# Modulation columns by transposes, and up products over high and low activations side by side

## The chip, the cores and the metric

One NeuronCore of one Trainium2 chip runs the whole program. The metric is the device time of one execution in microseconds (us), the median of several runs.

## What is computed

Two transformer blocks of two layers each, on 256 tokens of 1024 features, all in float32. The part that the change touches is the MLP, which stands in each of the four layers (and once more for the context stream of the second block, five in all), and the modulation of the second block:

```python
def hybrid_layer(...):                       # first block, two layers
    ...
    u = rms_norm(x, ln2) @ w_up              # 1024 -> 4096
    return x + jnp.square(jax.nn.relu(u)) @ w_down

def second_block(x, c, ctx, c_ctx, ...):     # two layers
    ctx_s = ctx
    for l in range(DEPTH):
        mod = (jax.nn.silu(c) @ w_mod[l] + b_mod[l])[:, None, :]
        mod_c = (jax.nn.silu(c_ctx)[None] @ w_mod[l] + b_mod[l])[:, None, :]
        sh1, sc1, gt1, sh2, sc2, gt2 = jnp.split(mod, N_MOD, axis=-1)
        ...
        x = x + gt1 * merge_branches(...)
        x = x + gt2 * sq_relu_mlp(modulate(x, g_norm2[l], sh2, sc2), w_ff1[l], w_ff2[l])
```

## The kernel before

**Precision.** Every large product is made of three in a fast float32 format (`F32R`): a value is split into a high part, rounded to the format, and a low part, the rest. A weight chunk is one load of 1 MB (128 partitions x 2048 values) into one of six `RAW` buffers. ScalarE casts it to the high part in one of four `HI` buffers (line 619), VectorE subtracts to get the low part `LO` (line 1114), which overwrites `RAW`. Activations are kept as `AH` and `AL`, each 8 blocks of 128 features by 256 tokens. TensorE then adds high x high, high x low and low x high in PSUM.

**The MLP** (`mlp` on TensorE, ScalarE and VectorE) has four rounds i of eight chunks j. The chunks j = 0 to 3 hold up weights, 256 hidden features each. `features_out` makes them: two halves q of 128 features, and for each the 8 blocks of input features, three products of 256 columns (lines 1805 to 1807), into half a PSUM bank, 4 or 5 in turn. ScalarE takes the relu (line 751) and its square, rounded, as `HIDH`; VectorE takes relu times value as `U2` and the rest as `HIDL` (lines 1231, 1235). The chunks j = 4 to 7 hold down weights, each 24 products of 512 columns (`tokens_out`, lines 1763 to 1765). `PS` is the whole of PSUM, eight banks of 512 values a partition. For early input of the next stage banks 6 and 7 take transposes in round 3.

**Order.** Each engine's program is written out by hand. At each chunk c ScalarE and VectorE first run `ahead(c)`, the split of chunk c + 3, and then the work on what TensorE made of chunk c. `s_used` counts chunks that TensorE has ended, `s_lo` splits that are done, `s_ufree` banks that are free, `s_hl` low parts of hidden features. SyncE issues the load of chunk c + 6 when chunk c is used.

**Modulation.** 24 groups of 512 columns of `w_mod`. `mod_chunk` (line 1838, or `modulation`, line 1972) makes two rows (the two streams) in one bank with four column tiles: the 1024 input features are spread over them, so that rows 0 and 1 of each of four blocks of 32 partitions hold partial sums. ScalarE copies the bank to `ROWS` or `ROWS4`. Then `mod_column` (line 1846) makes columns of them: four products of `ROWS` with the constant selector `SEL` (128 x 2), which adds the four blocks and leaves 2 columns for each 128 features, 8 in one bank. VectorE adds the bias into `MOD` (line 1187). Two groups come before a stage, two or three in the second block's gate chunks, one in some MLPs; at the end of each layer of the first block four come together, all in bank 3, behind the first half group of the output projection `c_o` (lines 2077 to 2082 on TensorE, 1467 to 1473 on VectorE), with TensorE waiting for `s_modc` before the third.

The selector is the last of twelve constants that ScalarE loads before its first work.

Of the kernel before, what the change touches and what calls it, by code (L numbers as in the profile page):

```python
# [15 lines left out]
P = 128  # L16
D = 1024
KT = D // P
# [117 lines left out]
MT_BANK = (1, 0, 1)  # L136

# [72 lines left out]
def build(nc, a, out):  # L210

    with ExitStack() as ctx:
# [20 lines left out]
        AH = sb("AH", [P, KT, S], F32R)  # L233
        AL = sb("AL", [P, KT, S], F32R)
# [20 lines left out]
        SEL = sb("SEL", [P, 2])  # L255
# [141 lines left out]
        s_so = sem("output_gate")  # L397
        s_rl = sem("hidden_relu")
# [114 lines left out]
        NCH = LP.end  # L513

# [102 lines left out]
        def _(act):  # L617
# [29 lines left out]
            const(SEL[:, :], a["selector"])  # L647
# [40 lines left out]
            def high(n, scale=None, shift=None, steps=range(4)):  # L688

                for s in steps:  # L690
                    act.wait_ge(s_tp, n + s - steps[0] + 1)
                    dst = AH[:, 2 * s:2 * s + 2, :].rearrange("p a n -> p (a n)")
                    if scale is None:
                        cast(dst, PS[:, 6 + s % 2, :]).then_inc(s_thi, 1)
                        continue

                    whole = vector_scales(s, shift)
                    out = dst if whole else TMP[:, s % 2, :]
                    for j in range(2):
                        last = nc.scalar.activation(out[:, 256 * j:256 * j + 256],  # L700
# [3 lines left out]
                    if whole:  # L704
                        last.then_inc(s_thi, 1)
                    else:
                        link(last)
                        cast(dst, TMP[:, s % 2, :]).then_inc(s_thi, 1)
# [22 lines left out]
            def mlp(q, c, u, late=NO_SLOT):  # L731

                e = EARLY.get(q)
                for i in range(4):
                    for j in range(8):
                        ahead(c + 8 * i + j + late.n)
# [11 lines left out]
                        if j < 4:  # L748

                            act.wait_ge(s_used, c + 8 * i + j + late.n + 1 + HL_N)  # L750
                            nc.scalar.activation(RL[:, j % 2, :], PS[:, 4 + (u + j) % 2, :], ACT.Relu).then_inc(s_rl, 1)  # L751
# [343 lines left out]
        def _(dve):  # L1095
# [34 lines left out]
            def low(n, scale=None, shift=None, steps=range(4)):  # L1130

                for s in steps:
                    d = 2 * s
                    hi = AH[:, d:d + 2, :].rearrange("p a n -> p (a n)").bitcast(F32)
                    lo = AL[:, d:d + 2, :].rearrange("p a n -> p (a n)")

                    dve.wait_ge(s_thi, n + s - steps[0] + 1)
                    full = PS[:, 6 + s % 2, :] if scale is None else TMP[:, s % 2, :]
                    if scale is not None and shift is not None and vector_scales(s, shift):
# [4 lines left out]
                    if scale is not None and shift is None:  # L1144
                        for j in range(2):
                            last = stt(lo[:, 256 * j:256 * j + 256], PS[:, 6 + s % 2, 256 * j:256 * j + 256],
                                       scale(d + j), hi[:, 256 * j:256 * j + 256], ALU.mult, ALU.subtract)
# [36 lines left out]
            def mod_column(g, bank):  # L1184

                l, k = g // 12, 4 * (g % 12)
                tt(MOD[:, l, k:k + 4, :], PS[:, bank, 0:8].rearrange("p (c s) -> p c s", s=2),
                   PAR[:, 128 + 48 * l + k:132 + 48 * l + k].unsqueeze(2).to_broadcast((P, 4, 2)),
# [20 lines left out]
            def mlp(q, c, u, m, later=None):  # L1209

                e = EARLY.get(q)
                for i in range(4):
                    for j in range(8):
                        ahead(c + 8 * i + j + m.n)
# [11 lines left out]
                        if j < 4:  # L1226
# [25 lines left out]
            for l in range(DEPTH):  # L1252
# [443 lines left out]
        def _(pe):  # L1696
# [112 lines left out]

            def group(g, c, n=512):  # L1810
# [31 lines left out]

# [511 lines left out]
```

## Time and profile before

| | |
|---|---|
| median of 3 runs | 1882.28 us (1881.24 to 1882.91) |
| the profiled execution | 1882.55 us |
| its span, first to last instruction | 1880.7 us |
| TensorE busy | 1816.5 us, 97% |
| VectorE, ScalarE busy | 1104.7 us, 59%; 916.1 us, 49% |
| granted clock of TensorE, mean | 0.987 of full |
| moved by DMA | 342.49 MB, mean 182 GB/s |

Busy time of TensorE overlaps from one matmul to the next: the time between two starts is shorter than the duration that is printed. In names of the trace the two activation buffers are AH and AL. A matmul in plain float32, such as one with `SEL`, stands as two records. A window's clock is a share of full speed, 2.4 GHz; 0.50 is the lower level, 1.2 GHz.

### The profile page before, as it was taken

What the parts mean: (1) busy time and instruction counts of PE and PEld (TensorE: products, weight loads), DVE (VectorE), ACT (ScalarE), POOL (GpSimd) and SP (SyncE); (2) the same over time, 40 slices, a digit from 0 to 9 for tenths busy, and PEclk for the clock granted to TensorE, in tenths of its full rate; (3) what the DMA queues carried; (4) which work ended last, traced back from release to release, by engine and by line L of the source; (5) the groups of instructions that cost most, each with busy time, mean ns of one, the idle gap of its engine ahead of it and who ended that gap; (6) DMA issues with size and microseconds to landing.
All of it is one profiled execution on the core that took longest, in us unless ns stands there. A gap on an engine that the chain in (4) does not pass through costs nothing.

```text
span 1880.7 us, 26344 instructions
## 1 busy us (share of the span) xinstructions
PE 1816.5 (97%) x11210; PEld 1562.8 (83%) x11210; DVE 1104.7 (59%) x1247; ACT 916.1 (49%) x1211; POOL 38.4 (2%) x32
## 2 busy tenths in 40 slices
PE   7899999998899999999999999999999999999998
PEld 6768999796689998778899997778999787779997
DVE  3866555466655545357655564686555655676554
ACT  5454444453454445465544544555444545654442
POOL 0000000000000000000000000000000000000000
PEclk9999999999999999999999999999999999999999
DMA  7464565653656657564656555636565656355562
GB/s 245 135 207 152 186 195 180 219 161 125 215 178 187 194 179 247 201 207 142 212 185 195 180 180 196 206 113 202 183 195 183 224 165 216 113 179 157 180 195 73
DMA packets 228236, 342.49 MB, mean 182 GB/s; under 512 B 9908, under 2 KB 118808, under 8 KB 227992
## 3 DMA queue, kind: packets, MB, share of 16 engines
q1 hardware_dynamic: 226928, 339.45, 55.5%
q8 instruction: 89, 1.46, 0.3%
q10 hardware_dynamic: 1192, 1.36, 0.2%
q14 instruction: 27, 0.22, 0.0%
HBM read 339.74 MB, written 1.05 MB: 181 GB/s over the span
## 4 chain that ended last, share of the span: by engine, by line
PE 91%; DVE 5%; ACT 2%; issue 1%; POOL 1%; ACTq 0%; DVEq 0%; POOLq 0%
PE PS L1763 15%; PE PS L1765 14%; PE PS L1764 14%; PE PS L1805 9%; PE PS L1806 9%; PE PS L1807 9%; PE PS L2131 1%; PE PS L2179 1%; PE PS L2133 1%; PE PS L2132 1%; PE PS L2202 1%; PE PS L2190 1%; PE PS L1838 1%; PE PS L2151 1%; PE PS L2149 1%
## 5 line engine op out<-in xcount | busy, mean ns | idle before, releaser
L1114 DVE TENSOR_TENSOR LO<-RAW,HI 128x2048 fp32r<-128x2048 f32 (+1 forms) x274 | 621.4, 2276 | 413.6 <-ACT HI L619 412.8
L619 ACT CAST HI<-RAW 128x2048 fp32r<-128x2048 f32 (+1 forms) x274 | 516.5, 1891 | 266.4 <-PE PS L1765 225.6
L1805 PE MATMUL PS<-AH,HI 128*128 128x256 f32 x1424 | 409.3, 287 | 9.0 <-DVE AL L1561 7.9
L1806 PE MATMUL PS<-AL,HI 128*128 128x256 f32 x1424 | 407.9, 286 | 0.0
L1807 PE MATMUL PS<-AH,LO 128*128 128x256 f32 x1424 | 407.6, 286 | 0.0
L1805 PEld LDWEIGHTS PS<-AH,HI 128*128 128x128 f32 x1424 | 278.7, 196 | 11.3 <-issue 9.8
L1806 PEld LDWEIGHTS PS<-AL,HI 128*128 128x128 f32 x1424 | 278.6, 196 | 0.6
L1807 PEld LDWEIGHTS PS<-AH,LO 128*128 128x128 f32 x1424 | 278.4, 196 | 0.0
L1763 PE MATMUL PS<-HI,AH 128*128 128x512 f32 (+2 forms) x704 | 257.7, 366 | 0.0
L1765 PE MATMUL PS<-HI,AL 128*128 128x512 f32 (+2 forms) x704 | 252.0, 358 | 0.0
L1764 PE MATMUL PS<-LO,AH 128*128 128x512 f32 (+2 forms) x704 | 251.6, 357 | 0.0
L1763 PE MATMUL PS<-HI,HIDH 128*128 128x512 f32 x640 | 250.1, 391 | 0.0
L1764 PE MATMUL PS<-LO,HIDH 128*128 128x512 f32 x640 | 249.3, 389 | 0.0
L1765 PE MATMUL PS<-HI,HIDL 128*128 128x512 f32 x640 | 249.1, 389 | 0.0
L1763 PEld LDWEIGHTS PS<-HI,AH 128*128 128x128 f32 x704 | 137.6, 195 | 32.4 <-issue 14.3
L751 ACT ACTIVATE RL<-PS 128x512 f32<-128x512 f32 x80 | 47.8, 597 | 221.6 <-PE PS L1807 217.7
L1765 PEld LDWEIGHTS PS<-HI,AL 128*128 128x128 f32 x704 | 137.3, 195 | 19.1
L1764 PEld LDWEIGHTS PS<-LO,AH 128*128 128x128 f32 x704 | 137.8, 196 | 17.9 <-issue 0.5
L1765 PEld LDWEIGHTS PS<-HI,HIDL 128*128 128x128 f32 x640 | 120.2, 188 | 25.0
L1763 PEld LDWEIGHTS PS<-HI,HIDH 128*128 128x128 f32 x640 | 120.2, 188 | 24.2
L1764 PEld LDWEIGHTS PS<-LO,HIDH 128*128 128x128 f32 x640 | 120.3, 188 | 24.1
L1231 DVE SCALAR_TENSOR_TENSOR U<-PS,RL 128x512 f32<-128x512 f32 x80 | 55.3, 691 | 89.0 <-ACT RL L751 88.8
(269 smaller groups left out, 1862.4 us busy)
## 6 DMA issues: line engine op xcount, KB each, us to landing
RAW<-in_w_ff SPq DMA_DIRECT2D x96, 1024.0 KB, 5.4
RAW<-in_w_in SPq DMA_DIRECT2D x80, 1024.0 KB, 5.2
RAW<-in_w_mod SPq DMA_DIRECT2D x48, 1024.0 KB, 5.1
RAW<-in_w_up SPq DMA_DIRECT2D x32, 1024.0 KB, 5.5
RAW<-in_w_down SPq DMA_DIRECT2D x32, 1024.0 KB, 5.0
RAW<-in_w_o SPq DMA_DIRECT2D x12, 1024.0 KB, 5.0
RAW<-in_w_out SPq DMA_DIRECT2D x8, 1024.0 KB, 5.6
RAW<-in_w_attn_out SPq DMA_DIRECT2D x6, 1024.0 KB, 5.3
```

The costliest lines, as they stand in the source:

```text
L619: return nc.scalar.copy(dst, src)
L751: nc.scalar.activation(RL[:, j % 2, :], PS[:, 4 + (u + j) % 2, :], ACT.Relu).then_inc(s_rl, 1)
L1114: tt(LO[:, c % RAW_N, 0:n], RAW[:, c % RAW_N, 0:n], HI[:, NTH[c] % HL_N, 0:n].bitcast(F32), ALU.subtract).then_inc(s_lo, 1)
L1231: stt(U2[:, j % 2, :], PS[:, 4 + (u + j) % 2, :], 0.0, RL[:, j % 2, :], ALU.max, ALU.mult).then_inc(s_ufree, 1)
L1763: mm(o, th, hi[:, j, :], start=first and j == 0, stop=False)
L1764: mm(o, th, lo[:, j, :], start=False, stop=False)
L1765: ins = mm(o, tl, hi[:, j, :], start=False, stop=last and j == kt - 1)
L1805: mm(o, wh, ah[:, j, :], start=j == 0, stop=False)
L1806: mm(o, wh, al[:, j, :], start=False, stop=False)
L1807: ins = mm(o, wl, ah[:, j, :], start=False, stop=j == KT - 1)
L1838: last = mm(PS[32 * k:32 * k + 32, banks[j // 2], :], C32[:, 4 * (j % 2) + k, :], RAW[:, c % RAW_N, 512 * k:512 * k + 512], start=j % 2 == ...
L2131: mm(o, th, hi[:, j, cols], start=j == 0, stop=False)
```

## The change

1. `AH` and `AL` become two views of one tensor `AHL`, in which each block of features has its 256 high values and then its 256 low ones.
2. In each MLP all up chunks but the first two of round 0 use `features_wide`: per block of features one product of the high weights with the 512 columns of `AHL`, and one of the low weights with the 256 high columns, added to the first half of the bank. Each half q of the chunk has a bank of its own: 6 and 7 for even j, 4 and 5 for odd.
3. ScalarE copies the first halves of both banks to `U2` before it runs `ahead`, VectorE adds the second halves and frees the banks; relu and square then read `U2`.
4. `mod_column` transposes the four pieces of a row group with the identity into the whole bank, and VectorE sums the four blocks in a reduction and adds the bias. At the layers' ends the four groups go to banks 4, 5, 3 and 2. The selector and its load are gone.

```diff
+TAIL_BANKS = (4, 5, 3, 2)
...
-        AH = sb("AH", [P, KT, S], F32R)
-        AL = sb("AL", [P, KT, S], F32R)
+        AHL = sb("AHL", [P, KT, 2, S], F32R)
+        AH, AL = AHL[:, :, 0, :], AHL[:, :, 1, :]
...
+        def wide(i, j):
+
+            return i > 0 or j > 1
+
+        def copies(q, i, j):
+
+            return 14 * q + 4 * i + j - 1
+
+        def wide_banks(j):
+
+            return 4 if j % 2 else 6
...
-            const(SEL[:, :], a["selector"])
...
+                        if j < 4 and wide(i, j):
+
+                            b = wide_banks(j)
+                            act.wait_ge(s_used, c + 8 * i + j + late.n + 1 + HL_N)
+                            act.wait_ge(s_hl, 16 * q + 4 * i + j - 1)
+                            cast(U2[:, j % 2, :].rearrange("p (a n) -> p a n", a=2),
+                                 PS[:, b:b + 2, 0:256]).then_inc(s_up, 1)
                         ahead(c + 8 * i + j + late.n)
...
 
-                            act.wait_ge(s_used, c + 8 * i + j + late.n + 1 + HL_N)
-                            nc.scalar.activation(RL[:, j % 2, :], PS[:, 4 + (u + j) % 2, :], ACT.Relu).then_inc(s_rl, 1)
+                            if wide(i, j):
+                                act.wait_ge(s_ufree, u + 4 * i + j + 1 + 2)
+                                up = U2[:, j % 2, :]
+                            else:
+                                act.wait_ge(s_used, c + 8 * i + j + late.n + 1 + HL_N)
+                                up = PS[:, 4 + (u + j) % 2, :]
+                            nc.scalar.activation(RL[:, j % 2, :], up, ACT.Relu).then_inc(s_rl, 1)
                             act.wait_ge(s_rl, 16 * q + 4 * i + j + 1)
                             nc.scalar.activation(HIDH[:, j // 2, 2 * (j % 2):2 * (j % 2) + 2, :].rearrange("p a n -> p (a n)"),
                                                  RL[:, j % 2, :], ACT.Square).then_inc(s_hh, 1)
...
                 l, k = g // 12, 4 * (g % 12)
-                tt(MOD[:, l, k:k + 4, :], PS[:, bank, 0:8].rearrange("p (c s) -> p c s", s=2),
-                   PAR[:, 128 + 48 * l + k:132 + 48 * l + k].unsqueeze(2).to_broadcast((P, 4, 2)),
+                mod = MOD[:, l, k:k + 4, :]
+                parts = PS[:, bank, :].rearrange("p (c b r) -> p c r b", c=4, b=4)[:, :, 0:2, :]
+                link(nc.vector.tensor_reduce(mod, parts, AX_X, ALU.add))
+                tt(mod, mod, PAR[:, 128 + 48 * l + k:132 + 48 * l + k].unsqueeze(2).to_broadcast((P, 4, 2)),
                    ALU.add).then_inc(s_modc, 1)
 
...
                     for j in range(8):
+                        if j < 4 and wide(i, j):
+
+                            b = wide_banks(j)
+                            dve.wait_ge(s_up, copies(q, i, j))
+                            up = U2[:, j % 2, :].rearrange("p (a n) -> p a n", a=2)
+                            tt(up, up, PS[:, b:b + 2, 256:512], ALU.add).then_inc(s_ufree, 1)
                         ahead(c + 8 * i + j + m.n)
...
                             dve.wait_ge(s_rl, 16 * q + 4 * i + j + 1)
-                            stt(U2[:, j % 2, :], PS[:, 4 + (u + j) % 2, :], 0.0, RL[:, j % 2, :], ALU.max,
-                                ALU.mult).then_inc(s_ufree, 1)
-                            dve.wait_ge(s_ufree, u + 4 * i + j + 1 + 2)
+                            if wide(i, j):
+                                link(stt(U2[:, j % 2, :], U2[:, j % 2, :], 0.0, RL[:, j % 2, :], ALU.max, ALU.mult))
+                            else:
+                                stt(U2[:, j % 2, :], PS[:, 4 + (u + j) % 2, :], 0.0, RL[:, j % 2, :], ALU.max,
+                                    ALU.mult).then_inc(s_ufree, 1)
+                                dve.wait_ge(s_ufree, u + 4 * i + j + 1 + 2)
                             dve.wait_ge(s_hh, 16 * q + 4 * i + j + 1)
                             tt(HIDL[:, j // 2, cols:cols + 2, :].rearrange("p a n -> p (a n)"),
...
-                dve.wait_ge(s_mcol, L.m_o.g + 4)
                 for j in range(4):
-                    g = L.m_o.g + j
-                    tt(MOD[:, g // 12, 4 * (g % 12):4 * (g % 12) + 4, :],
-                       PS[:, 3, 8 * j:8 * j + 8].rearrange("p (c s) -> p c s", s=2),
-                       PAR[:, 128 + 48 * (g // 12) + 4 * (g % 12):132 + 48 * (g // 12) + 4 * (g % 12)].unsqueeze(2)
-                       .to_broadcast((P, 4, 2)), ALU.add).then_inc(s_modc, 1)
+                    dve.wait_ge(s_mcol, L.m_o.g + j + 1)
+                    mod_column(L.m_o.g + j, TAIL_BANKS[j])
                 gain = lambda k: PAR[:, 16 + 8 * l + k:17 + 8 * l + k]
...
+            def features_wide(c, b):
+
+                arrived(c)
+                hi, lo = slot(c, KT, 256)
+                for q in range(2):
+                    for j in range(KT):
+                        wh, wl = hi[:, j, 128 * q:128 * q + 128], lo[:, j, 128 * q:128 * q + 128]
+                        mm(PS[:, b + q, :], wh, AHL[:, j, :, :].rearrange("p a n -> p (a n)"), start=j == 0, stop=False)
+                        ins = mm(PS[:, b + q, 0:256], wl, AH[:, j, :], start=False, stop=j == KT - 1)
+                ins.then_inc(s_used, 1)
+
             def group(g, c, n=512):
...
+            def turn_rows(rows, bank):
+
+                for k in range(4):
+                    last = nc.tensor.transpose(PS[:, bank, 128 * k:128 * k + 128], rows[:, 128 * k:128 * k + 128], IDM)
+                last.then_inc(s_mcol, 1)
+
             def mod_column(j, bank):
 
-                for k in range(4):
-                    last = mm(PS[:, bank, 2 * k:2 * k + 2], ROWS[:, j, 128 * k:128 * k + 128], SEL[:, :],
-                              start=True, stop=True)
-                last.then_inc(s_mcol, 1)
+                turn_rows(ROWS[:, j, :], bank)
 
             def mod_columns(m, banks):
...
-                        features_out(c + 8 * i + j + (0 if first else m.n), 4 + (u + j) % 2, AH, AL,
-                                     ts if first else None, tiles if first else None, 1 + m.n if first else 1)
+                        if wide(i, j):
+                            features_wide(c + 8 * i + j + m.n, wide_banks(j))
+                        else:
+                            features_out(c + 8 * i + j + (0 if first else m.n), 4 + (u + j) % 2, AH, AL,
+                                         ts if first else None, tiles if first else None, 1 + m.n if first else 1)
                         if i == 0 and j == 1:
...
+                        if e and i == 3 and j == 0:
+                            pe.wait_ge(s_ufree, u + 4 * i + 2 + 1 + 2)
...
                     pe.wait_ge(s_mrow, L.m_o.g + j + 1)
-                    for k in range(4):
-                        last = mm(PS[:, 3, 8 * j + 2 * k:8 * j + 2 * k + 2], ROWS4[:, j, 128 * k:128 * k + 128],
-                                  SEL[:, :], start=True, stop=True)
-                    last.then_inc(s_mcol, 1)
+                    turn_rows(ROWS4[:, j, :], TAIL_BANKS[j])
                 half_group(L.c_o + 1, 0, 1, ts=ts)
```

How it stands in the order of the instructions, in three places.

TensorE at the start of an up chunk in layer 0's MLP (j = 2 of round 0), before; `AH` and `AL` are the activations:

```order
L1805 MATMUL PS<-AH,HI 128x256 [waits chunk_split_done,ubank_evacuated]
L1806 MATMUL PS<-AL,HI 128x256
L1807 MATMUL PS<-AH,LO 128x256
L1805 MATMUL PS<-AH,HI 128x256
L1806 MATMUL PS<-AL,HI 128x256
```

and in the changed program, the end of that chunk and the start of the next (j = 3):

```order
L1849 MATMUL PS<-AHL,HI 128x512
L1850 MATMUL PS<-AHL,LO 128x256
L1849 MATMUL PS<-AHL,HI 128x512 [waits chunk_split_done,ubank_evacuated]
L1850 MATMUL PS<-AHL,LO 128x256
L1849 MATMUL PS<-AHL,HI 128x512
L1850 MATMUL PS<-AHL,LO 128x256
```

The triple of 256 columns has become a pair of 512 and 256, and what a chunk waits for is the same.

ScalarE in the same round, before (j = 2 and 3):

```order
L619 CAST HI<-RAW 128x2048 [waits chunk_used,raw_loaded_4]
L751 ACTIVATE RL<-PS 128x512 [waits chunk_used]
L753 ACTIVATE HIDH<-RL 128x512 [waits hidden_relu]
L619 CAST HI<-RAW 128x2048 [waits chunk_used,raw_loaded_5]
L751 ACTIVATE RL<-PS 128x512 [waits chunk_used]
L753 ACTIVATE HIDH<-RL 128x512 [waits hidden_relu]
```

and now; `U_104` is `U2`:

```order
L632 COPY U_104<-PS 128x512 [waits hidden_low,chunk_used]
L632 CAST HI<-RAW 128x2048 [waits chunk_used,raw_loaded_5]
L775 ACTIVATE RL<-U_104 128x512 [waits ubank_evacuated]
L777 ACTIVATE HIDH<-RL 128x512 [waits hidden_relu]
L632 COPY U_104<-PS 128x512 [waits hidden_low,chunk_used]
L632 CAST HI<-RAW 128x2048 [waits chunk_used,raw_loaded_0]
L775 ACTIVATE RL<-U_104 128x512 [waits ubank_evacuated]
L777 ACTIVATE HIDH<-RL 128x512 [waits hidden_relu]
```

The copy out of the banks stands ahead of the split of a later chunk, which used to come before anything that waits for this chunk; the relu waits for VectorE.

TensorE at the end of layer 0, before: the last of the four groups of modulation columns (three like it stand above) and the start of the next half group of `c_o`; `ROWS_104` is `ROWS4`:

```order
L2080 MATMUL PS<-SEL,ROWS_104 128x2 [waits mod_rows_copied]
L2080 MATMUL PS<-SEL,ROWS_104 128x2 x3
L1763 MATMUL PS<-HI,AH 128x512 [waits activation_low,chunk_split_done]
L1764 MATMUL PS<-LO,AH 128x512
L1765 MATMUL PS<-HI,AL 128x512
```

and now, `CT` being the identity and `ROWS_102` the same `ROWS4`:

```order
L1889 MATMUL PS<-CT,ROWS_102 128x128 [waits mod_rows_copied]
L1889 MATMUL PS<-CT,ROWS_102 128x128 x3
L1795 MATMUL PS<-HI,AHL 128x512 [waits activation_low,chunk_split_done]
L1796 MATMUL PS<-LO,AHL 128x512
L1797 MATMUL PS<-HI,AHL 128x512
```

Sixteen transposes stand where the sixteen selector products stood.

## Rows read from the trace of the kernel before

**Rows 1.** The page before: parts 1 (busy us, share, instructions), 2 and 4.

```profile
PE 1816.5 (97%) x11210; PEld 1562.8 (83%) x11210; DVE 1104.7 (59%) x1247; ACT 916.1 (49%) x1211; POOL 38.4 (2%) x32
...
PEclk9999999999999999999999999999999999999999
...
PE 91%; DVE 5%; ACT 2%; issue 1%; POOL 1%; ACTq 0%; DVEq 0%; POOLq 0%
```

**Rows 2.** Timeline of ScalarE in an MLP: start us, us, engine line op out<-in.

```profile
1001.53 0.60 ACT L751 ACTIVATE RL<-PS 128x512 f32<-128x512 f32 x1 [3.79 <-PE PS L1807]
1002.16 0.63 ACT L753 ACTIVATE HIDH<-RL 128x512 fp32r<-128x512 f32 x1
1002.70 1.89 ACT L619 CAST HI<-RAW 128x2048 fp32r<-128x2048 f32 x1
1007.29 0.60 ACT L751 ACTIVATE RL<-PS 128x512 f32<-128x512 f32 x1 [2.70 <-PE PS L1807]
...
1029.77 1.91 ACT L619 CAST HI<-RAW 128x2048 fp32r<-128x2048 f32 x1 [3.53 <-PE PS L1765]
1035.21 1.91 ACT L619 CAST HI<-RAW 128x2048 fp32r<-128x2048 f32 x1 [3.53 <-PE PS L1765]
```

**Rows 3.** The same of VectorE.

```profile
1004.62 2.29 DVE L1114 TENSOR_TENSOR LO<-RAW,HI 128x2048 fp32r<-128x2048 f32 x1 [1.04 <-ACT HI L619]
1007.92 0.69 DVE L1231 SCALAR_TENSOR_TENSOR U<-PS,RL 128x512 f32<-128x512 f32 x1 [1.00 <-ACT RL L751]
1008.65 0.69 DVE L1235 TENSOR_TENSOR HIDL<-U,HIDH 128x512 fp32r<-128x512 f32 x1
```

**Rows 4.** Timeline of TensorE and VectorE around the modulation columns, x records.

```profile
150.93 3.63 PE L2080 MATMUL PS<-SEL,ROWS 128*128 128x2 f32 x32
154.42 0.48 PE L1763 MATMUL PS<-HI,AH 128*128 128x512 f32 x1
...
380.42 1.84 PE L1846 MATMUL PS<-SEL,ROWS 128*128 128x2 f32 x16
...
497.58 4.26 PE L2080 MATMUL PS<-SEL,ROWS 128*128 128x2 f32 x32
501.70 0.77 PE L1763 MATMUL PS<-HI,AH 128*128 128x512 f32 x1
...
501.87 0.38 DVE L1470 TENSOR_TENSOR MOD<-PS,PAR 128x8 f32<-128x8 f32 x4 [3.81 <-PE PS L2080]
...
515.27 1.03 PE L1735 MATMUL PS<-CT,X 128*128 128x128 f32 x8
...
800.02 0.95 PE L1846 MATMUL PS<-SEL,ROWS 128*128 128x2 f32 x8
```

**Rows 5.** Busy time by windows: us, PE, PEld, DVE, ACT, POOL, PEclk, DMA share, GB/s.

```profile
155.60:159.00 3.40, 3.40 (x9) 2.66 (x9) 1.58 (x1) 0.00 (x0) 0.00 (x0) 0.50 0.10 31
...
500.30:507.10 6.80, 6.80 (x22) 5.64 (x22) 2.58 (x5) 0.00 (x0) 0.00 (x0) 0.51 0.57 191
380.40:384.00 3.60, 3.60 (x33) 3.60 (x32) 0.33 (x2) 3.35 (x5) 0.00 (x0) 1.00 0.62 185
515.00:516.10 1.10, 1.10 (x11) 0.97 (x10) 0.71 (x1) 0.14 (x1) 0.00 (x0) 1.00 0.55 193
1289.00:1296.00 7.00, 6.20 (x30) 6.23 (x31) 7.00 (x5) 5.02 (x5) 0.00 (x0) 0.52 0.00 0
```

**Rows 6.** Timeline of SyncE's queue and of ScalarE at the end of layer 1.

```profile
501.94 0.37 SPq L581 DMA_DIRECT2D CTX<-in_ctx  x1
502.35 8.04 SPq L550 DMA_DIRECT2D RAW<-in_w_up  x3
...
510.56 1.91 ACT L619 CAST HI<-RAW 128x2048 fp32r<-128x2048 f32 x1 [10.83 <-DMA RAW<-in_w_up]
```

**Rows 7.** Timeline of the opening.

```profile
5.88 0.37 ACTq L633 DMA_DIRECT2D SEL<-selector  x1
6.29 1.28 ACT L684 ACT_TABLE_LOAD   x1 [6.29 <-issue]
```

More of the change, by code:

```diff
@@ L254, in build @@
         C32 = sb("C32", [P, KT, 32])
-        SEL = sb("SEL", [P, 2])
         SGC = sb("SGC", [P, 16])
@@ L397, in build @@
         s_so = sem("output_gate")
+        s_up = sem("hidden_part_copied")
         s_rl = sem("hidden_relu")
@@ L691, in high @@
                     act.wait_ge(s_tp, n + s - steps[0] + 1)
-                    dst = AH[:, 2 * s:2 * s + 2, :].rearrange("p a n -> p (a n)")
+                    dst = AH[:, 2 * s:2 * s + 2, :]
                     if scale is None:
-                        cast(dst, PS[:, 6 + s % 2, :]).then_inc(s_thi, 1)
+                        cast(dst, PS[:, 6 + s % 2, :].rearrange("p (a n) -> p a n", a=2)).then_inc(s_thi, 1)
                         continue
                     whole = vector_scales(s, shift)
-                    out = dst if whole else TMP[:, s % 2, :]
+                    out = dst if whole else TMP[:, s % 2, :].rearrange("p (a n) -> p a n", a=2)
                     for j in range(2):
-                        last = nc.scalar.activation(out[:, 256 * j:256 * j + 256],
+                        last = nc.scalar.activation(out[:, j, :],
                                                     PS[:, 6 + s % 2, 256 * j:256 * j + 256], ACT.Identity,
@@ L707, in high @@
                         link(last)
-                        cast(dst, TMP[:, s % 2, :]).then_inc(s_thi, 1)
+                        cast(dst, out).then_inc(s_thi, 1)
             def copy_group(pair, c, dst, n):
@@ L1133, in low @@
                     d = 2 * s
-                    hi = AH[:, d:d + 2, :].rearrange("p a n -> p (a n)").bitcast(F32)
-                    lo = AL[:, d:d + 2, :].rearrange("p a n -> p (a n)")
+                    hi = AH[:, d:d + 2, :].bitcast(F32)
+                    lo = AL[:, d:d + 2, :]
                     dve.wait_ge(s_thi, n + s - steps[0] + 1)
                     full = PS[:, 6 + s % 2, :] if scale is None else TMP[:, s % 2, :]
+                    full = full.rearrange("p (a n) -> p a n", a=2)
                     if scale is not None and shift is not None and vector_scales(s, shift):
@@ L1145, in low @@
                         for j in range(2):
-                            last = stt(lo[:, 256 * j:256 * j + 256], PS[:, 6 + s % 2, 256 * j:256 * j + 256],
-                                       scale(d + j), hi[:, 256 * j:256 * j + 256], ALU.mult, ALU.subtract)
+                            last = stt(lo[:, j, :], PS[:, 6 + s % 2, 256 * j:256 * j + 256], scale(d + j), hi[:, j, :],
+                                       ALU.mult, ALU.subtract)
                         last.then_inc(s_tlo, 1)
@@ L2325, in _ @@
                 mlp(q.mlp, q.c_mlp, q.u + 3, q.m_mlp, None, tiles=q.tile(1, 1, 0))
-N_CONST, N_ROWS = 12, 11
+N_CONST, N_ROWS = 11, 11
 INPUTS = ["x", "ln1", "w_in", "conv_w", "conv_b", "igate_b", "fgate_b", "mlstm_norm", "moba_q_norm", "moba_k_norm",
@@ L2347 @@
     args["constants"] = nc.dram_tensor("constants", table.shape, F32, kind="ExternalInput").ap()
-    pairs = np.tile(np.eye(32, 2, dtype=np.float32), (4, 1))
-    arrays["selector"] = pairs
-    args["selector"] = nc.dram_tensor("selector", pairs.shape, F32, kind="ExternalInput").ap()
     out = nc.dram_tensor("out", (1, S, D), F32, kind="ExternalOutput").ap()
```

## The prediction, made before the changed kernel ran

> **What bounds the kernel now.** I read the page first: TensorE is busy 97% of the span, VectorE 59%, ScalarE 49%, and the chain that ended last is 91% TensorE; the granted clock is near full in all slices [rows 1]. So a TensorE instruction that disappears is worth its own start-to-start time wherever TensorE isn't waiting, and work added to VectorE and ScalarE is free until it makes TensorE wait.
>
> Second, the timeline of ScalarE in one MLP, since its waits on TensorE mark where each weight chunk ends. Two relus stand 5.76 us apart, two casts of the down half 5.44 us apart [rows 2]. An up chunk is 48 matmuls of 256 columns, so 5.76/48 = 0.120 us each; a down chunk is 24 of 512 columns, so 5.44/24 = 0.2267 us each. Doubling the columns costs 0.1067 us (256 columns at the full level, 2.4 GHz), so both sizes carry the same 0.0133 us that doesn't depend on columns. The durations printed (0.28, 0.39 us) overlap and are not the cost; the spacing is.
>
> Third, the timeline of VectorE in the same place: per up chunk one LO subtraction of 2.29 us, the squared relu 0.69, the low part 0.69, with waits between [rows 3]. That is 3.7 of 5.76 us; ScalarE has 0.60 + 0.63 + 1.89 = 3.1.
>
> Fourth, TensorE around the modulation columns, and the granted clock there by windows [rows 4, 5].
>
> **The change, part by part.**
>
> *Wide up products.* In each MLP 14 of 16 up chunks become wide (all but i = 0, j = 0 and 1), 5 MLPs, 70 chunks. Before: 16 triples of 256 columns, 48 x 0.120 = 5.76. Now: 16 products of 512 columns and 16 of 256, in alternation, as the order shows. The columns streamed are the same 12,288; what goes is 16 fixed parts. Chunk: 16 x (0.2267 + 0.120) = 5.55 us, 0.213 less; 70 x 0.213 = **14.9 us**. The trace of before has no alternation of the two sizes. Bounds: a pair costs at most what the triple does, 0.360 (no gain), or at least its columns without a fixed part, 0.320 (0.64 us a chunk, 45 us in all). I take 0.3467, since both neighbours show the same fixed part [rows 2].
>
> *What the wide products add.* ScalarE copies one half out of two banks (nearest: relu of the same size, 0.60 us), VectorE adds the other (nearest: 0.69 us) [rows 2, 3]: 42 us and 48 us in all, at zero, because TensorE covers them. The check: TensorE may overwrite a bank pair only after the addition, two chunks later. Behind the end of a chunk come the copy 0.60 and the addition 0.69, some 1.4 us, plus at worst one LO subtraction that VectorE has in hand, 2.29: 3.7 us against 5.55 us of cover. The weights: ScalarE now waits for chunk c before it casts c+3, where before it had cast c+3 while c ran. Queued behind that wait are the HI cast (1.89) and then LO (2.29), so c+3 is ready about 0.6 + 1.9 + 2.3 = 4.8 us after c ends; TensorE wants it 11.1 us after. VectorE per wide chunk: 0.69 + 2.29 + 0.69 + 0.69 = 4.4 of 5.55. ScalarE: 3.7. If this cover went, TensorE would stop at the bank pair of the next wide chunk.
>
> *Modulation columns.* 24 groups. Each was four products with the selector, which the trace counts as 8 records (192 records for 96); now four transposes, which elsewhere are one record each. Eight transposes print 1.03 us where eight selector records print 0.95, sixteen 1.84 and 32 print 3.63 [rows 4]; 32 end 3.49 us on by the next start, so 0.14 of each print is overlap. One record or one transpose costs about 0.11 either way, and half the records is half the time. Ten single groups: 0.81 less half of 0.89, 0.365 each, 3.7 us. Three pairs: 1.70 - 0.89 = 0.81 each, 2.4 us. Two sets of four at the layers' ends: 3.49 - 1.78 = 1.71 each, 3.4 us. Sum **9.5 us**. Bounds: nothing gained, if a transpose of these rows costs two records, to 10.5 us, at 0.10 a transpose. On VectorE each group gains a reduction of 32 elements a partition and a link; four additions took 0.38 us together [rows 4], so I put a group at 0.3 us, anywhere from 0.1 to the 0.69 of a 512-column operation. Hidden: TensorE asks for the columns only after a half group of 5.44 us.
>
> *The clock at the layers' ends.* Right behind the 32 selector records the granted clock falls to its lower level, 1.2 GHz: from 155.6 to 159.0 us in layer 0, and from 500.3 to 507.1 us in layer 1, with TensorE busy all along [rows 5]. Half the stretch is lost: 1.7 and 3.4 us (in layer 1 that includes the 0.63 us by which its 32 records took longer, 4.12 against 3.49). What TensorE did before the fall was 3.5 us of two-column products. In the place where it did only 1.7 us of them, the clock stayed full [rows 4, 5]. The change leaves 1.78 us of 128-column transposes, so I take both falls as gone: **5.1 us**. Bounds: 0, and -5.1 if they get twice as long.
>
> *DMA queues.* SyncE holds the context's load and three w_up loads behind the last column of layer 1 [rows 6]; this comes 4.12 - 1.78 = 2.3 us earlier, and so do they. The cast of the second up chunk waited for that load until 510.56. TensorE ends the half group before it at 497.58 + 1.78 + 5.44 = 504.8, so the wait survives and lasts to about 508.3. It costs nothing: the cast and LO are done at 508.3 + 1.9 + 2.3 = 512.5, and TensorE gets to this chunk after two more half groups, eight transposes and a quarter of a chunk, at 504.8 + 10.9 + 0.9 + 1.4 = 518. The selector's load was the last of ScalarE's twelve, 0.41 us before its first activation [rows 7]; without it the opening is at most **0.4 us** earlier, at least 0 if x lands no sooner. I take 0.4.
>
> **Sum.** 14.9 + 9.5 + 5.1 + 0.4 = 29.9 us off the profiled execution's own 1882.55 us (span 1880.7 and 1.85 around it): **1852.6**. The median of the three runs, 1882.28, is 0.3 us lower, far inside the error. Stretches at the lower clock also stand behind waits at the passes' ends (1289 to 1296: mean clock 0.52 [rows 5]); they may shift with all that moves, each worth about 1.7 us, and I allow 3.5 us both ways.
>
> **Rivals.**
>
> *A, the clock still falls at the layers' ends.* No row shows sixteen transposes in one run between half groups. The sum loses 5.1: 1857.7. For it: the run of narrow work is halved, not gone. Against: eight selector pairs' worth, 1.7 us, and eight transposes leave the clock at full [rows 5].
>
> *B, wide products save nothing.* A pair costs 0.360, because a short product can't cover the fixed part of a long one. 1852.6 + 14.9 = 1867.5. Against: the equal fixed part at both sizes.
>
> *C, slower: transposes throw the clock down.* Columns are turned in 15 places, and each would then be followed by a stretch like layer 0's, 3.4 us long, 1.7 lost: 25.5 us. The transposes themselves would stream at half pace and gain nothing. 1882.55 - 14.9 - 0.4 + 25.5 = 1892.8. It decides from 9 of 15 places (9 x 1.7 = 15.3, what else is gained). Against it: at 515.27 eight transposes stand between half groups, and the clock of their window is 1.00 [rows 4, 5].
>
> The Trainium skill (TensorE: Matmul & The Clock Gate, Part 4: PE-mode transpose) states that full clock does not engage for transposes, which it says are not counted as busy in the same way. By that rule this change would trade one poor filler for another, and rival A or even C would hold. The trace does not bear out its strong form. No row says whether it holds weakly.
>
> *D, slower: the bank pairs.* If copy and addition ended later than the next chunk, TensorE would wait at each of 70 wide chunks. From 5.55 us on it costs; it eats all other gains from 6.0 us on (29.9/70 = 0.43). At 7 us it costs 1.45 x 70 = 101 us: 1852.6 + 101 = 1954. Worked out above at 3.7 at most, so it needs a stall that no row shows.
>
> That the change doesn't do what it says is excluded by the order: 70 chunks are in alternation and the selector has gone.
>
> **How the numbers follow.** The forecast 0.67; A 0.17; B 0.06; C 0.03; D 0.02; a small new wait somewhere of 3 to 8 us, 0.05. A measurement of this kernel tells about 0.2%, 3.8 us, from no change. All but C and D are faster by more; for the same I leave 0.01, for slower 0.05, faster 0.94. The range: from 1847 (the forecast with the clock kinder by 3.5 and a fixed part that shrinks a little) to 1862 (A with a small wait); B, C and D lie outside, some 0.12 to 0.15 with the tails. The one result above 1862 that I count likeliest is B.
>
> **What would show it.** Relus in the i = 1 rounds 5.55 us apart; 1120 products of 512 columns and 1120 of 256 in the new line, no wait of TensorE on the addition; 96 records of ROWS transposes, four in some 0.44 us; granted clock 1.00 in the windows behind them; an addition of about 0.69 us on VectorE and a copy of 0.60 on ScalarE, 70 of each. Wrong would be: a spacing of 5.7 or more (B), clock 0.5 behind the turned rows (A or C), TensorE idle before a wide chunk (D).

## The result, and the profile after

The changed kernel takes **1861.51 us** (median of 4 runs, 1859.63 to 1862.39), the kernel before 1882.57 us beside it (4 runs, 1881.24 to 1882.91): a ratio of 0.9888, interval 0.9871 to 0.9905. That is faster, by 21 us where 29.9 were forecast; the predicted time was 1852.6, the range 1847 to 1862. The profiled execution took 1862.11 us, its span 1860.3; against the 1882.55 from which the sum was made that is 20.4 us less.

The page of the changed kernel, the lines that answer to [rows 1], and from its part 5 the costliest groups of the new code (busy us, mean ns of one | idle before, releaser):

```profile
PE 1796.1 (97%) x9994; PEld 1488.6 (80%) x9994; DVE 1148.0 (62%) x1341; ACT 950.2 (51%) x1281; POOL 38.4 (2%) x32
...
PEclk9999999899999999999999999999999999999999
...
PE 89%; DVE 6%; ACT 2%; issue 1%; POOL 1%; DMA 1%; ACTq 0%; DVEq 0%; POOLq 0%
...
L1849 PE MATMUL PS<-AHL,HI 128*128 128x512 f32 x1120 | 396.2, 398 | 0.0
L1850 PE MATMUL PS<-AHL,LO 128*128 128x256 f32 x1120 | 314.3, 281 | 0.0
...
L632 ACT COPY U<-PS 128x512 f32<-128x512 f32 x70 | 41.1, 587 | 260.4 <-PE PS L1850 260.4
...
L1246 DVE TENSOR_TENSOR U<-U,PS 128x512 f32<-128x512 f32 x70 | 48.2, 688 | 136.8 <-ACT U L632 136.6
```

The change does what it says: 1120 wide and 1120 narrow products, 70 copies of 587 ns, 70 additions of 688 ns. TensorE has no idle time ahead of either product (0.0), so the 89 us of new work on ScalarE and VectorE cost nothing in the MLPs. Two things already differ from the plan: VectorE has 6% of the chain of waits where it had 5, and one slice of the granted clock shows an 8 where before none did.

The timeline of ScalarE in the same MLP as [rows 2] (start us, us, engine line op):

```profile
987.73 0.59 ACT L632 COPY U<-PS 128x512 f32<-128x512 f32 x1 [9.12 <-PE PS L1850]
988.21 1.91 ACT L632 CAST HI<-RAW 128x2048 fp32r<-128x2048 f32 x1
990.02 0.63 ACT L775 ACTIVATE RL<-U 128x512 f32<-128x512 f32 x1
990.68 0.63 ACT L777 ACTIVATE HIDH<-RL 128x512 fp32r<-128x512 f32 x1
993.38 0.59 ACT L632 COPY U<-PS 128x512 f32<-128x512 f32 x1 [2.06 <-PE PS L1850]
...
999.04 0.59 ACT L632 COPY U<-PS 128x512 f32<-128x512 f32 x1 [2.08 <-PE PS L1850]
```

The copies, each released by a chunk's last product, are 5.65 us apart: neither the 5.55 of the forecast nor the 5.76 of before. That is 5.65/16 = 0.3531 us a pair; from the second pair of a chunk on, three pairs take 1.06 us in nearly all chunks, 0.3533 each. And of TensorE itself:

```profile
1000.84 0.28 PE L1850 MATMUL PS<-AHL,LO 128*128 128x256 f32 x1
1000.96 0.40 PE L1849 MATMUL PS<-AHL,HI 128*128 128x512 f32 x1
1001.20 0.28 PE L1850 MATMUL PS<-AHL,LO 128*128 128x256 f32 x1
1001.31 0.40 PE L1849 MATMUL PS<-AHL,HI 128*128 128x512 f32 x1
```

From a wide start to the next narrow start it is 0.24 us here, from a narrow one to the next wide one 0.11 (over all 70 chunks 0.2361 and 0.1168 in the mean). The first was taken as 0.2267, the second as 0.120: the wide product's place grew by 9 ns, the narrow one's shrank by 3.

The turned rows, at the ends of layers 0 and 1 and before the second attention part of pass 1, with the one instruction in the span that now waits for a modulation column:

```profile
151.38 1.91 PE L1889 MATMUL PS<-CT,ROWS 128*128 128x128 f32 x16
153.04 0.48 PE L1795 MATMUL PS<-HI,AHL 128*128 128x512 f32 x1
...
492.02 1.91 PE L1889 MATMUL PS<-CT,ROWS 128*128 128x128 f32 x16
493.68 0.48 PE L1795 MATMUL PS<-HI,AHL 128*128 128x512 f32 x1
...
703.23 1.04 PE L1889 MATMUL PS<-CT,ROWS 128*128 128x128 f32 x8
...
711.11 0.39 PE L1837 MATMUL PS<-AHL,HI 128*128 128x256 f32 x1 [1.10 <-DVE MOD L1215]
```

Sixteen transposes take 1.66 us to the next start; in [rows 4] the 32 selector records took 3.49 and 4.12. The last row is the small new wait that the prediction gave 0.05: TensorE stands 1.10 us. VectorE's timeline says why:

```profile
708.16 2.29 DVE L1138 TENSOR_TENSOR LO<-RAW,HI 128x2048 fp32r<-128x2048 f32 x1 [1.30 <-ACT HI L632]
710.37 0.18 DVE L1214 TENSOR_REDUCE MOD<-PS 128x8 f32<-128x32 f32 x1
710.59 0.17 DVE L1215 TENSOR_TENSOR MOD<-MOD,PAR 128x8 f32<-128x8 f32 x1
710.67 0.18 DVE L1214 TENSOR_REDUCE MOD<-PS 128x8 f32<-128x32 f32 x1
710.89 0.17 DVE L1215 TENSOR_TENSOR MOD<-MOD,PAR 128x8 f32<-128x8 f32 x1
```

Before, it did the same work as two additions:

```profile
720.07 2.29 DVE L1114 TENSOR_TENSOR LO<-RAW,HI 128x2048 fp32r<-128x2048 f32 x1 [0.72 <-ACT HI L619]
722.27 0.23 DVE L1187 TENSOR_TENSOR MOD<-PS,PAR 128x8 f32<-128x8 f32 x2
```

The four small operations are cheap, but they are queued behind the split of a weight chunk, and its cast had waited for the load:

```profile
706.22 1.91 ACT L632 CAST HI<-RAW 128x2048 fp32r<-128x2048 f32 x1 [1.68 <-DMA RAW<-in_w_in]
```

TensorE gets to this product 13.0 us earlier than before; the split starts 11.9 us earlier, and the columns are ready (711.06 against 722.50) only 11.4 us earlier, since VectorE's own part grew from 0.23 to 0.69 us. Before, TensorE took the product at 722.88, 0.4 us behind the additions, so it didn't stop.

The granted clock (windows: us, PE, PEld, DVE, ACT, POOL, PEclk, DMA share, GB/s), where [rows 5] had 0.50 and 0.51 behind the selector products:

```profile
136.00:140.00 4.00, 4.00 (x23) 1.88 (x26) 1.64 (x4) 2.37 (x5) 0.00 (x0) 0.59 0.69 239
151.00:158.00 7.00, 7.00 (x41) 6.04 (x40) 4.51 (x10) 1.91 (x1) 0.00 (x0) 1.00 0.52 152
491.00:504.00 13.00, 13.00 (x68) 10.99 (x67) 8.64 (x13) 2.31 (x2) 0.00 (x0) 1.00 0.70 237
1471.00:1475.00 4.00, 3.51 (x17) 3.52 (x18) 2.40 (x5) 3.55 (x10) 0.00 (x0) 0.57 1.09 362
```

Behind both sets of transposes it is now full. But it falls to the lower level, 1.2 GHz, at 136 us, in layer 0's attention part. There the kernel before had the full one:

```profile
136.00:140.00 4.00, 3.96 (x34) 2.37 (x34) 2.59 (x6) 3.29 (x10) 0.00 (x0) 1.00 0.78 277
```

### The profile page after: what moved, and what is told of

Same layout as the page of the kernel before. It is cut to its first block, busy times and chain, and to the rows that moved or that the text cites. A ratio compares the mean times of both kernels' runs of the same rounds, so it can differ in the third digit from the quotient of the medians.

```text
span 1860.3 us, 24145 instructions
## 1 busy us (share of the span) xinstructions
PE 1796.1 (97%) x9994; PEld 1488.6 (80%) x9994; DVE 1148.0 (62%) x1341; ACT 950.2 (51%) x1281; POOL 38.4 (2%) x32
## 4 chain that ended last, share of the span: by engine, by line
PE 89%; DVE 6%; ACT 2%; issue 1%; POOL 1%; DMA 1%; ACTq 0%; DVEq 0%; POOLq 0%
PE PS L1795 14%; PE PS L1796 14%; PE PS L1797 14%; PE PS L1849 14%; PE PS L1850 7%; PE PS L1837 2%; PE PS L1838 2%; PE PS L1839 2%; DVE LO L1138 1%; PE PS L2179 1%; PE PS L2227 1%; PE PS L2181 1%; PE PS L2180 1%; PE PS L2250 1%; PE PS L2238 1%
## 5 line engine op out<-in xcount | busy, mean ns | idle before, releaser
L1849 PE MATMUL PS<-AHL,HI 128*128 128x512 f32 x1120 | 396.2, 398 | 0.0
L1850 PE MATMUL PS<-AHL,LO 128*128 128x256 f32 x1120 | 314.3, 281 | 0.0
L1795 PE MATMUL PS<-HI,AHL 128*128 128x512 f32 (+2 forms) x704 | 256.2, 364 | 0.0
L1849 PEld LDWEIGHTS PS<-AHL,HI 128*128 128x128 f32 x1120 | 210.4, 188 | 51.8
L1797 PE MATMUL PS<-HI,AHL 128*128 128x512 f32 (+2 forms) x704 | 250.5, 356 | 0.0
L1796 PE MATMUL PS<-LO,AHL 128*128 128x512 f32 (+2 forms) x704 | 250.5, 356 | 0.0
L1850 PEld LDWEIGHTS PS<-AHL,LO 128*128 128x128 f32 x1120 | 211.5, 189 | 0.6
L1795 PEld LDWEIGHTS PS<-HI,AHL 128*128 128x128 f32 x704 | 136.8, 194 | 32.2 <-issue 14.3
L1797 PEld LDWEIGHTS PS<-HI,AHL 128*128 128x128 f32 x704 | 136.8, 194 | 18.7
L1796 PEld LDWEIGHTS PS<-LO,AHL 128*128 128x128 f32 x704 | 136.9, 194 | 17.4 <-issue 0.5
L1246 DVE TENSOR_TENSOR U<-U,PS 128x512 f32<-128x512 f32 x70 | 48.2, 688 | 136.8 <-ACT U L632 136.6
L1837 PE MATMUL PS<-AHL,HI 128*128 128x256 f32 x304 | 92.5, 304 | 9.3 <-DVE AHL L1593 7.9
L1838 PE MATMUL PS<-AHL,HI 128*128 128x256 f32 x304 | 91.0, 299 | 0.0
```

The costliest lines, as they stand in the source:

```text
L1246: tt(up, up, PS[:, b:b + 2, 256:512], ALU.add).then_inc(s_ufree, 1)
L1795: mm(o, th, hi[:, j, :], start=first and j == 0, stop=False)
L1796: mm(o, th, lo[:, j, :], start=False, stop=False)
L1797: ins = mm(o, tl, hi[:, j, :], start=False, stop=last and j == kt - 1)
L1837: mm(o, wh, ah[:, j, :], start=j == 0, stop=False)
L1838: mm(o, wh, al[:, j, :], start=False, stop=False)
```

## Where the 20.4 us lie

The two traces hold the same first products of the down halves (high weights by `HIDH`), so the lead of the changed kernel can be read at the same piece of work:

| first down product of | before | after | lead, us |
|---|---|---|---|
| layer 0 | 199.06 | 195.85 | 3.21 |
| layer 1 | 547.29 | 536.49 | 10.80 |
| the third MLP | 928.97 | 915.72 | 13.25 |
| the fourth | 1316.38 | 1300.00 | 16.38 |
| the fifth | 1718.39 | 1699.35 | 19.04 |
| the last down product's start | 1874.41 | 1854.05 | 20.36 |

Within each MLP, from the first down product to the fourth round's, the lead grows by 1.32 us in twelve wide chunks (0.110 each), and nothing else happens there. Read from the products just ahead of and behind each place, the terms are:

| term | forecast | measured |
|---|---|---|
| 70 wide chunks | 14.9 | 70 x (1.32 / 12) = 7.7 |
| columns, 10 singles | 3.7 | 8 x 0.35 + 2 x 0.46 = 3.7 |
| 3 pairs | 2.4 | 3 x (1.705 - 0.79) = 2.7 |
| 2 sets of four | 3.4 | 2 x (3.49 - 1.66) = 3.7 |
| the new wait | 0 | -1.4 |
| falls of the clock at the layers' ends | 5.1 | 1.6 + 3.2 = 4.8 |
| a fall at 136 us | 0 | -1.5 |
| a fall at 1471 us | 0 | -0.5 |
| opening | 0.4 | 0.5 + 0.6 = 1.1 |
| sum | 29.9 | 20.3, of 20.4 |

Each of the lower lines is a step of the lead. At layer 0's end the lead goes from -0.45 (150.24 before, 150.69 after) over the columns to 1.38 (154.42, 153.04) and over the fall to 3.01 (161.59, 158.58). At layer 1's end it goes over the fall from 8.02 (501.70, 493.68) to 10.6, and the 0.63 us by which the slow clock had stretched the 32 records belong to it. Around the attention part of pass 1 that has the new wait the lead loses 0.46 though a pair gains 0.91, so the wait costs 1.4 with the 1.10 of idle time in it. Across the fall at 1471 the lead goes from 17.68 (1450.84, 1433.16) to 17.21 (1496.42, 1479.20). In the opening TensorE starts 0.5 us earlier, and its products of 256 columns go from a spacing of 0.21 to one of 0.12 us at 30.9 us instead of 32.8, which is worth another 0.6. What is left are small steps of both signs.

## Experiments

Batches of four kernels ran on one chip each, with the kernel before among them: 1883.95 us (7 runs) for the first four, 1885.23 (9 runs) for the last four.

**The columns alone.** All up chunks as triples of 256 columns; the wait for a bank pair that only wide chunks need goes too.

```diff
-            return i > 0 or j > 1
+            return False
...
-                        if e and i == 3 and j == 0:
-                            pe.wait_ge(s_ufree, u + 4 * i + 2 + 1 + 2)
```

> Only the transposed columns; all up chunks as before. The terms for the columns say 10 x 0.32 (spacing measured in the changed kernel) + 3 x 0.81 + 2 x 1.71 = 9.0 us and 0.4 at the opening, so 1873 with no help from the clock. If the 32 two-column records were what threw the clock down at the layers' ends, both falls are gone here too and it is near 1868. If the falls only come with the timing of the moment, one or both may stand there still, or others turn up elsewhere, and the time lies anywhere from 1868 to 1875.

Measured 1868.44 us (1866.21 to 1869.0), ratio 0.9917 (0.9902 to 0.9931): 15.5 us, near the forecast's 9.5 + 5.1 + 0.4 = 15.0 (a single column group gains 0.35 here as in the changed kernel, not the 0.32 of the expectation, and a pair 0.91). The windows of this kernel:

```profile
151.00:158.00 7.00, 7.00 (x41) 6.04 (x40) 5.21 (x10) 1.92 (x2) 0.00 (x0) 1.00 0.51 152
491.00:504.00 13.00, 13.00 (x67) 10.99 (x67) 9.72 (x14) 4.30 (x3) 0.00 (x0) 1.00 0.48 163
```

So the columns' and the clock's terms were about right, and the missing part is to be sought in the wide products. That the sum comes out so near is in part luck: 2.6 us of this profile's lead come at 1280 to 1291 us, where its clock is 1.00 and that of before is 0.52 ([rows 5], 1289 to 1296), and 1.5 us go to a fall at 131 us. The wait at the second attention part is here too (0.98 us, on the same line of VectorE).

**The wide products alone.** Selector, its products and the additions from them as before.

```diff
-                    last = nc.tensor.transpose(PS[:, bank, 128 * k:128 * k + 128], rows[:, 128 * k:128 * k + 128], IDM)
+                    last = mm(PS[:, bank, 2 * k:2 * k + 2], rows[:, 128 * k:128 * k + 128], SEL[:, :],
+                              start=True, stop=True)
```

> Only the wide products; columns with the selector as before. At the spacing of 0.3533 us a pair that the changed kernel shows, 16 x 70 x (0.360 - 0.3533) = 7.5 us: 1875. At the 0.3467 that was forecast, 14.9 us: 1867.6. If the two-column records throw the clock down, the two falls at the layers' ends are back.

Measured 1873.09 us (1872.78 to 1874.51), ratio 0.9945 (0.993 to 0.996): 10.9 us less. A chunk takes 5.65 us as in the changed kernel (slots 0.2361 and 0.1168), which is 7.7 us. Part of the rest is the clock: this profile too has 1.00 where the one of before has its fall at 1289 us, which gives 2.6, and it has a fall of its own at 137 us, which takes 1.6. No product waits for a modulation column. And the falls are back, here from the timeline and the windows at the layers' ends:

```profile
152.00 4.47 PE L1888 MATMUL PS<-SEL,ROWS 128*128 128x2 f32 x32
156.34 0.77 PE L1794 MATMUL PS<-HI,AHL 128*128 128x512 f32 x1
```

```profile
155.00:162.00 7.00, 7.00 (x22) 5.81 (x23) 2.58 (x5) 0.00 (x0) 0.00 (x0) 0.54 0.27 93
500.00:507.00 7.00, 7.00 (x23) 5.85 (x23) 2.58 (x5) 0.00 (x0) 0.00 (x0) 0.56 0.57 201
```

With the selector the clock falls in both places, without it in neither; the same holds in all ten profiles (two with the selector, eight with transposes). This kernel has the fall at 137 us as well, so a fall there doesn't take the place of the one at 155. So these falls belong to the two-column products. Whether their two columns or their plain float32 form counts isn't shown.

**Eight wide, then eight narrow.** The same products, grouped; each half chunk is 8 wide, 8 narrow, 8 wide, 8 narrow.

```diff
-                    for j in range(KT):
-                        wh, wl = hi[:, j, 128 * q:128 * q + 128], lo[:, j, 128 * q:128 * q + 128]
-                        mm(PS[:, b + q, :], wh, AHL[:, j, :, :].rearrange("p a n -> p (a n)"), start=j == 0, stop=False)
-                        ins = mm(PS[:, b + q, 0:256], wl, AH[:, j, :], start=False, stop=j == KT - 1)
+                    for j0 in range(0, KT, 8):
+                        for j in range(j0, j0 + 8):
+                            wh = hi[:, j, 128 * q:128 * q + 128]
+                            mm(PS[:, b + q, :], wh, AHL[:, j, :, :].rearrange("p a n -> p (a n)"), start=j == 0, stop=False)
+                        for j in range(j0, j0 + 8):
+                            wl = lo[:, j, 128 * q:128 * q + 128]
+                            ins = mm(PS[:, b + q, 0:256], wl, AH[:, j, :], start=False, stop=j == KT - 1)
```

> The changed kernel, but in each half chunk the eight wide products stand in a row, then the eight narrow ones. If the loss (0.3533 for a pair against 0.2267 + 0.120) comes from the alternation of long and short products, the wide ones run at 0.2267 and the narrow ones at 0.120, a chunk takes 5.55 us, and the kernel is 7 us faster than the changed one (1854.5). If it comes from the wide product itself (two halves of one bank, or both parts of AHL), the wide ones stay at 0.233 or more in a row, a chunk takes 5.65 us, and the time is 1861.5.

Measured 1855.73 us (1853.88 to 1857.1), ratio 0.9851 (0.9836 to 0.9865). Its TensorE:

```profile
230.08 2.00 PE L1850 MATMUL PS<-AHL,HI 128*128 128x512 f32 x8
231.92 1.12 PE L1853 MATMUL PS<-AHL,LO 128*128 128x256 f32 x8
232.87 2.00 PE L1850 MATMUL PS<-AHL,HI 128*128 128x512 f32 x8
```

Eight pairs take 232.87 - 230.08 = 2.79 us, 0.3488 a pair and 5.58 a chunk: 0.0045 of the 0.0066 between 0.3533 and 0.3467. Most of the extra time is gone when the sizes don't alternate. What stays is in the wide ones: eight take 1.84 us, 0.230 each, where 0.2267 was expected, and eight narrow ones 0.95, 0.119 each.

**Two wide, two narrow.** As above with 2 in place of 8.

> As the last, in runs of two wide and two narrow products. If each change between long and short costs 0.0067 us, half of the changes are gone and the kernel is about 3.7 us faster than the changed one (1857.8). If it is not the alternation, nothing moves (1861.5).

Measured 1854.24 us (1851.13 to 1859.5), ratio 0.9853 (0.9834 to 0.9871).

```profile
190.33 0.63 PE L1850 MATMUL PS<-AHL,HI 128*128 128x512 f32 x2
190.80 0.39 PE L1853 MATMUL PS<-AHL,LO 128*128 128x256 f32 x2
191.03 0.63 PE L1850 MATMUL PS<-AHL,HI 128*128 128x512 f32 x2
```

Two pairs in 0.70 us, 0.3484 a pair over all chunks. Groups of 2 change size four times as often as groups of 8 and are no slower, so it isn't a price per change of size, as the expectation's 3.7 us had it.

**The changed kernel and the grouping by two, again,** on another chip beside each other.

> The changed kernel once more, beside the next ones on one chip: 1861 to 1863. It is there for the comparison. Where its profile has stretches at the lower clock, they need not stand where they stood in the first profile, if their place is chance; if the two-column records were their cause, none stands behind the turned rows at the layers' ends.

> The version in runs of two wide and two narrow products, again, to settle its size. A pair took 0.3484 us there against 0.3533, so 16 x 70 x 0.0049 = 5.5 us less than the changed kernel, if the clock falls as often in both. If the 7 to 9 us seen before come back in the mean, the clock has a part in them.

Measured 1862.08 us (1860.82 to 1864.16), ratio 0.9885 (0.9871 to 0.9898), for the changed kernel, and 1855.08 (1851.72 to 1856.62), ratio 0.9841 (0.9827 to 0.9855), for the grouping: the intervals lie apart. Of the 7.0 us the chunks explain 70 x (5.65 - 16 x 0.3484) = 5.3. The rest is of the size by which runs of one kernel differ with their mean clock: the four of the first grouping by two went from 1851.13 us at 0.991 to 1859.5 at 0.986. The fall at 136 us is there again in the second profile of the changed kernel:

```profile
136.00:140.00 4.00, 4.00 (x22) 1.80 (x25) 1.41 (x4) 2.33 (x4) 0.00 (x0) 0.57 0.66 238
```

It is no constant of the transposes: the kernel with wide products alone has 0.69 in this window, the columns alone fall from 131, and the first profile of the grouping by two falls nowhere between 85 and 361 us though it has both parts.

**Each row turned three times.** The sets of four at the layers' ends become 48 transposes, into the same banks, ahead of the ones that count.

```diff
+                    for k in range(8):
+                        nc.tensor.transpose(PS[:, TAIL_BANKS[j], 128 * (k % 4):128 * (k % 4) + 128],
+                                            ROWS4[:, j, 128 * (k % 4):128 * (k % 4) + 128], IDM)
```

> The changed kernel, with each of the four groups at the layers' ends turned three times (twice for nothing): 48 transposes in one run, 5.3 us, more than the 3.5 us of two-column products that stood there. If transposes count for the clock as little as those did, the clock falls behind them, at about 155 and 497 us, for 3.4 us or more each, and the kernel is 7 us (2 x 3.55) plus 3 to 7 us slower than the changed one: 1872 to 1876. If they keep it up, it stays at 1.00 there and the time is 1861.5 + 7.1 = 1868.6.

Measured 1868.11 us (1866.89 to 1871.07), ratio 0.9918 (0.9904 to 0.9931): 6.0 above the changed kernel beside it, where 64 transposes at 0.108 are 6.9. The timeline gives 1.30 us for twelve (153.61 to 154.91), so 48 run for 5.2 us. The clock:

```profile
151.00:157.00 6.00, 6.00 (x45) 5.48 (x44) 2.92 (x6) 2.59 (x2) 0.00 (x0) 1.00 0.32 87
157.00:163.00 6.00, 6.00 (x38) 5.26 (x37) 2.92 (x5) 0.00 (x0) 0.00 (x0) 1.00 0.26 91
...
497.00:500.00 3.00, 3.00 (x26) 2.83 (x25) 1.52 (x3) 1.91 (x1) 0.00 (x0) 1.00 0.00 0
500.00:506.00 6.00, 6.00 (x43) 5.48 (x41) 3.27 (x7) 0.00 (x0) 0.00 (x0) 1.00 0.28 72
```

5.2 us of 128-column transposes, longer than the 3.5 us of two-column products, leave the clock full throughout and behind them. It isn't the length of the stretch without wide products that pulled the clock down, but what ran in it.

**One transpose ahead of each wide chunk,** to see whether a break alters the alternation.

```diff
+                nc.tensor.transpose(PS[:, b, 0:128], IDM, IDM)
```

> The changed kernel, with one transpose (0.11 us, its result is overwritten) ahead of each wide chunk. In two places of the changed kernel, behind the four turned rows of round 0 in the first two passes, a pair took 0.3467 us instead of 0.3533 for a whole chunk. If a short break at the start puts TensorE in that faster rhythm for the chunk, all wide chunks have 0.3467 here. If those two places have another reason, the spacing stays at 0.3533 and the kernel is 70 x 0.11 = 7.7 us slower, 1869.

Measured 1862.26 us, one run, no different from the changed kernel. A chunk takes 5.69 us with the transpose's 0.11 in it; from the second pair on the pairs are 0.3494 us apart in the mean. That mean mixes two paces: in 43 of the 70 chunks the pairs are 0.347 us apart, in 27 of them 0.354. The break brings most of what the grouping brings, and costs as much as it brings.

The changed kernel has both paces too. In 66 of its chunks the pairs are 0.353 to 0.354 us apart, but in four, those behind the single rows turned in the third and fourth MLP (904.5 and 1288.8 us) and the ones after them, it is 0.3467. The second of them in the fourth MLP, from its first product to the first down product:

```profile
1294.45 0.39 PE L1849 MATMUL PS<-AHL,HI 128*128 128x512 f32 x1
1294.68 0.27 PE L1850 MATMUL PS<-AHL,LO 128*128 128x256 f32 x1
...
1300.00 0.39 PE L1795 MATMUL PS<-HI,HIDH 128*128 128x512 f32 x1
```

5.55 us is the forecast's chunk, to the digit, in strict alternation and less than either grouping takes. So the alternation as such doesn't cost the 0.0066 us; it runs at one of two paces, nearly always at the slow one, and a break ahead of a chunk can put it into the fast one. What chooses the pace isn't shown.

## Why the prediction was right, and where it was off

The time, 1861.51, lies in the range by 0.5 us, and that is luck: the upper end, 1862, stood for A with a small wait, and A didn't come. The same kernel on the second chip took 1862.08. Of the 9.5 us that the sum was too high, 7.2 are of one term.

*The wide products: the term that was mis-sized.* The step was "both neighbours show the same fixed part", so that a pair costs 0.2267 + 0.120 = 0.3467. It costs 0.3533 nearly everywhere, within the stated bounds of 0.320 to 0.360 and halfway to rival B, and the term is 7.7 us instead of 14.9. Spacings measured in runs of equal products were added up for a run of alternating ones, which the trace of before did not contain. The difference is 2% of a pair, but half of a saving that was itself only 0.0133 of 0.36. Grouping by two takes away 0.0049 of the 0.0066 us, grouping by eight 0.0045. The sum of the two spacings can be reached: four of the 70 chunks have it.

*The cover.* Copy 0.59 and addition 0.69 were as forecast, and no product of a wide chunk waited. Rival D was rightly small, and the kernel with wide products alone has no wait of this kind either.

*The columns.* 10.1 measured, the wait apart, 9.5 forecast: right in all three kinds. A transpose is one record of about 0.104 us (1.66/16), a little less than the 0.11 that was taken, and a group on VectorE took 0.189 + 0.167 = 0.36 us, put at 0.3. Wrong was the sentence "TensorE asks for the columns only after a half group of 5.44 us": in one place of 15 the columns stand behind the split of a late weight chunk, and TensorE waited 1.10 us (0.23 to 1.61 in the kernels that have the new columns, nothing in the two that have the old). The forecast looked at the durations of the new operations and not at what is queued ahead of them where loads set the pace.

*The clock.* Both falls at the layers' ends are gone, as forecast; the pair of single-part kernels shows that the selector products made them, and with that rival A is out. They gave 4.8 of the 5.1. The net is less, since the clock also falls at 136 and at 1471 us, which costs 1.5 and 0.5. The prediction had allowed 3.5 us either way for such shifts. The opening gave 1.1 where at most 0.4 was stated: 0.6 of it is the spacing that went to 0.12 us at 30.9 us instead of 32.8. That is chance, for in the other kernels with the change it does so at 30.3 to 33.0 us.

*Transposes and the clock.* Rival C didn't come: the granted clock is 1.00 behind each of the 15 places. The Trainium skill (TensorE: Matmul & The Clock Gate, Part 4: PE-mode transpose) states that the full clock does not engage for transposes. With 5.2 us of them in one run the granted clock was 1.00 in every window, and behind them, so they didn't pull it down here. The measurement decides. The clock was already full ahead of each run of them; whether it would rise under transposes alone wasn't tried.

*The queue at layer 1's end.* The loads of `w_up` came earlier and the wait for them survived without cost, as forecast, here against [rows 6]:

```profile
494.44 5.34 SPq L563 DMA_DIRECT2D RAW<-in_w_up  x3
```

```profile
503.60 1.91 ACT L632 CAST HI<-RAW 128x2048 fp32r<-128x2048 f32 x1 [9.42 <-DMA RAW<-in_w_up]
```

The cast starts at 503.60, 4.7 us earlier than the forecast's 508.3: the three loads were also issued in 5.34 us instead of 8.04.

## What to carry to other kernels

The spacing of a product holds for the order in which it was measured. When a saving is a few per cent of the spacing, build the new order or give the forecast its full bounds: here 7 ns in 353 were half of the gain. Where products of two sizes go to the same accumulators, try two and two beside one and one: the best kernel of this study is the change with its products grouped by two, 1855.08 us beside 1862.08 and 1885.23. And a cheap operation that an otherwise idle engine gains is free only if nothing late stands ahead of it in the queue.

## What the runs showed of the chip

Strictly alternating products of 512 and 256 columns, each with weights of its own, have two paces: 0.3533 us by pairs in 66 of 70 chunks of the changed kernel, 0.3467 in four, and with a transpose ahead of each chunk 0.354 in 27 and 0.347 in 43. In groups of two a pair takes 0.3484, in groups of eight 0.3488; the sum of the spacings in uniform runs is 0.3467. Why is open: no run separated the weight loads from the products.

About 3.5 us of plain float32 products of two columns are followed by the lower clock while TensorE stays busy, in all four places of two profiles; 5.2 us of 128-column transposes are not.

Falls of the clock in the attention parts and at the passes' ends lie differently from one execution to the next, even of one kernel: added up over windows of 1 us, TensorE was at the lower level for 47.3 us in the first profile of the changed kernel and 48.6 in the second, 33.5 and 46.1 in the two of the grouping by two, and 48.4 in that of the kernel before. Half of such a total is at most what it costs, so single executions of one kernel can lie up to 6 us apart by this alone; these two of the grouping by two took 1851.13 and 1856.13 us. What decides where a fall comes was not tried.
